# Moving the resident weight tiles 576 bytes down in SBUF, and three small constants behind them

## The reference

```python
for i in range(DEPTH):                      # DEPTH = 2
    h = _rmsnorm(x, g_pre[i])
    o = even_mixer(h) if i % 2 == 0 else odd_mixer(h)
    x = x + _rmsnorm(o, g_post[i])
    x = x + jax.nn.sigmoid(x @ w_ple_gate[i]) * (p[i] @ w_ple[i])
```

## Time and profile before

| | |
|---|---|
| median of 3 runs | 1965.39 us (1963.24 to 1967.23) |
| the profiled execution | 1967.23 us, of which its span (first to last instruction) is 1965.4 us |
| TensorE clock granted, mean | 0.982 of 2.4 GHz |
| PE busy | 1885.1 us, 96% of the span, 9712 matmuls |
| PE weight loads | 1596.0 us, under the matmuls |
| DVE / ACT / POOL busy | 1207.4 / 729.4 / 783.1 us |
| DMA | 302.91 MB moved, 154 GB/s |

### The profile page before, as it was taken

The page is one execution under the profiler, slowest core; times in us unless marked ns, Lnnn a source line. Parts: engine busy times, 40 slices in busy tenths (PEclk is TensorE's granted clock), DMA queues, the critical chain, the costliest instruction groups (busy, mean ns, idle before and its releaser), DMA issues. The chain is left out here.

```text
span 1965.4 us, 26367 instructions
## 1 busy us (share of the span) xinstructions
PE 1885.1 (96%) x9712; PEld 1596.0 (81%) x9712; DVE 1207.4 (61%) x1827; ACT 729.4 (37%) x1471; POOL 783.1 (40%) x540
## 2 busy tenths in 40 slices
PE   4999999999989999999988999999989999999999
PEld 3788888888889788788877888877879889888887
DVE  5499999926678316513754200165667777688886
ACT  6111211211578432212322111122568787445432
POOL 0111121132587553454533322233588975254201
PEclk8999999999999999999989999999989999999999
DMA  4201432453576557544320222286545376557834
GB/s 168 71 11 51 150 99 91 137 170 112 170 251 225 169 170 251 186 131 137 126 63 24 77 86 78 71 335 187 182 153 216 122 259 240 189 192 243 297 128 146
DMA packets 145189, 302.91 MB, mean 154 GB/s; under 512 B 31601, under 2 KB 60017, under 8 KB 145074
## 3 DMA queue, kind: packets, MB, share of 16 engines
q1 hardware_dynamic: 145074, 301.39, 45.6%
HBM read 190.00 MB, written 111.35 MB: 153 GB/s over the span
## 5 line engine op out<-in xcount | busy, mean ns | idle before, releaser
L590 DVE SCALAR_TENSOR_TENSOR ie_acc<-ie_u,ie_wconv,ie_acc 128x1551 f32<-128x1551 f32 x120 | 250.2, 2085 | 3.2
L3039 PE MATMUL og_ps<-w_hi_part,bl_ring 128*128 128x512 f32 x672 | 217.8, 395 | 1.0 <-DVE bl_ring L2572 1.0
L188 POOL TENSOR_TENSOR w_lo_part<-w_raw,w_hi_part 128x1024 fp32r<-128x1024 f32 x24 | 65.3, 2720 | 329.7 <-ACT w_hi_part L180 329.7
L325 PE MATMUL ie_ps<-rows_hi,w_hi_part 128*128 128x512 f32 x384 | 151.0, 393 | 5.0 <-DVE w_lo_part L554 5.0
L325 PE MATMUL ie_ps<-rows_lo,w_hi_part 128*128 128x512 f32 x384 | 150.5, 392 | 0.0
L325 PE MATMUL ie_ps<-rows_hi,w_lo_part 128*128 128x512 f32 x384 | 150.3, 392 | 0.0
L3039 PEld LDWEIGHTS og_ps<-w_hi_part,bl_ring 128*128 128x128 f32 x672 | 126.9, 189 | 27.1 <-DVE bl_ring L2572 1.1
L170 POOL TENSOR_TENSOR w_hi_part<-w_raw,zero 128x1024 fp32r<-128x1024 f32 x40 | 77.7, 1942 | 167.2 <-DMA w_raw<-wall 164.8
L2459 DVE TENSOR_TENSOR mla_pt_lo<-mla_ps_t,mla_pt_hi 128x512 fp32r<-128x512 f32 x160 | 109.2, 687 | 42.2 <-ACT mla_pt_hi L2428 41.3
L3039 PE MATMUL og_ps<-w_lo_part,bl_ring 128*128 128x512 f32 x336 | 131.4, 391 | 0.0
L1859 DVE SCALAR_TENSOR_TENSOR io_stage<-io_tanh,io_ps 128x512 f32<-128x512 f32 x24 | 16.5, 688 | 174.1 <-ACT io_tanh L1817 174.1
(11 more groups left out here) (332 smaller groups left out, 5177.0 us busy)
## 6 DMA issues: line engine op xcount, KB each, us to landing
w_raw<-wall SPq DMA_DIRECT2D x68, 512.0 KB, 4.6
w_hi_part<-weight_blocks SPq DMA_DIRECT2D x28, 512.0 KB, 5.4
w_lo_part<-weight_blocks SPq DMA_DIRECT2D x28, 512.0 KB, 5.6
weight_blocks<-w_hi_part SPq DMA_DIRECT2D x26, 512.0 KB, 7.9
w_flat<-wall SPq DMA_DIRECT2D x16, 512.0 KB, 8.8
weight_blocks<-w_lo_part SPq DMA_DIRECT2D x16, 512.0 KB, 7.3
weight_blocks<-w_raw_rounded SPq DMA_DIRECT2D x14, 512.0 KB, 8.2
pro_x<-x SPq DMA_DIRECT2D x12, 512.0 KB, 8.6
```

What stands on the lines that cost most here:

```text
L325: mm = pe.matmul(psum[:, u % banks], w_at(g, name, a, k * HALF + c * P, P), g.XT[m][:, k, b * 512:(b + 1) * 512], start=i == 0, stop=i == ...
L590: dve.scalar_tensor_tensor(acc[:], ubuf[:, cc, s:s + CW], wconv[:, cc, s:s + 1], acc[:], ALU.mult, ALU.add).then_inc(taps, 1)
L3039: mm = pe.matmul(ps[:, N % 4], bl.part(a, N)[:, k], wb.at(N // HT, m, k), start=k + a + m == 0, stop=k == 3 and a == 1)
```

## The change

`g.W` is now taken with `g.sb` directly behind the staging tile, and `ident`, `zero` and `minus_half` come after it. Before they lay between the two. `g.base`, from which all later tiles are placed, is now computed from the next free offset.

```diff
+        w_at_byte = -(-nc.sbuf_base // 32) * 32
+        g.W = [g.sb("w_hi_part", [P, 2, PAIRCOLS], F32R), g.sb("w_lo_part", [P, 2, PAIRCOLS], F32R)]
+        g.W_flat = [g.region(w_at_byte + 8 * PAIRCOLS * i).sb(f"w_flat{i}", [P, 2, PAIRCOLS]) for i in range(2)]
         g.ident = g.sb("ident", [P, P])
         g.zero = g.sb("zero", [P, 1])
-        g.mhalf = g.sb("minus_half", [P, 1])
-        w_at_byte = -(-nc.sbuf_base // 32) * 32
-        w_at = g.region(w_at_byte)
-        g.W = [w_at.sb("w_hi_part", [P, 2, PAIRCOLS], F32R), w_at.sb("w_lo_part", [P, 2, PAIRCOLS], F32R)]
-        g.W_flat = [g.region(w_at_byte + 8 * PAIRCOLS * i).sb(f"w_flat{i}", [P, 2, PAIRCOLS]) for i in range(2)]
         g.zero3 = g.zero[:].rearrange("p (a b) -> p a b", a=1).broadcast_to([P, NT, DH])
...
+        g.mhalf = g.sb("minus_half", [P, 1])
...
-        g.base = w_at.at
+        g.base = -(-nc.sbuf_base // 32) * 32
```

## The result

The changed kernel is slower: 1984.55 us, median of four runs (1983.84 to 1985.62), against 1965.83 (1963.24 to 1967.23) for four of the kernel before. The ratio is 1.0097, 95% interval 1.008 to 1.0114. The forecast was no change, and its range of 1959 to 1972 does not hold the time. The profiled execution took 1981.16 us with a span of 1979.4, 14.0 us more than the span before.

What follows compares the result with a forecast made beforehand. TensorE, busy 96% of the span, was taken as the bound: matmul count times the distance between starts. Span 1965.4 us plus five terms of 0 gave a median of 1965.4 us, range 1959 to 1972.

Steps and rivals of the forecast that it cites:

- Steps 2 to 5: Transposes, VectorE's convolution steps, POOL's splits with their constant, and DMAs of the weight tiles: each forecast to add 0.
- step 1: TensorE matmuls with a weight tile as operand, at most 5880: 0 ns change each, bounds +6.3 and -13.6 ns.
- first rival: Products of weights and rows: unlike operand starts cost 6.3 ns in each of 5880, 37 us, giving 2002 us; chance 5%.
- Step 4: POOL's splits and the constant they read: 0, bounds 0 and +2 us; only splits at 1398.69 us on the chain.
- Three mixtures and one price: TensorE: 256 column products, transposes and Fourier products with differing start remainders were said to show no price for unlikeness.
- 13.6 ns beside the columns: TensorE: what each 512 column matmul takes (226.9 ns) above its columns' 213.3 ns; said to belong to the matmul.
- second rival: Weight matmuls: the old start at 192 causes their surplus; sparing all 13.6 ns saves 80 us, giving 1885 us; chance 4%.

## Why the prediction was wrong

The view of the bottleneck held: a count of matmuls times the distance between starts, and two thirds of them with a weight tile. Steps 2 to 5 held as well: transposes, DVE, POOL's constant and the DMAs cost nothing. The step that failed is step 1, the value of 0 ns per matmul. It was measured as 2.2 ns where the weights are stationary and 5 to 6.4 ns where they move, 23.4 us of TensorE's time and 18.7 us of the kernel's, inside the stated bounds of -13.6 and +6.3 but at the wrong end. So the first rival was the truth, with a chance of 5%, and its price of 37 us was too high by a factor of two, since matmuls with stationary weights paid a third of it and those of 480 columns and fewer nothing. Step 4 also read the chain too short: after the splits at 1398.69 us it runs through eight more POOL instructions, from 1414.37 us, that write `w_flat`, which is the moved memory. It did no harm, since the mean of its line 2644 is 2382 ns before and after.

Three arguments against that rival did not carry.

- The products of 256 columns and the transposes were taken as tests of unlike operands. They are not: transposes start 95.8 ns apart with their operands alike and 95.7 unlike, and the products of 256 columns in line 2226 went from 119.0 ns alike to 116.4 unlike. "Three mixtures and one price" compared shapes that do not show this price. The only rows of 512 columns with unlike remainders were the latents', and they were slow.
- The attention scores, alike and yet at 396 ns, were read as the same slowness from short groups. Short groups alone do not cost that: line 2257, with groups as short, fell to 227.1 and 227.6 ns as soon as its operands were alike. The scores keep 231 ns in every run here (230.7 to 231.1 on average), and why is open. They stand between products of line 2389 whose operands are unlike in every run (320 and 192 by 512), and lines 1666 and 3069 above are alike groups that rose beside unlike ones, so it may be the same cause at one remove; no run tested that.
- The 13.6 ns beside the columns were rightly put to the matmul and not to its start: no layout brought a line of 512 columns under 226.7 ns on average. The second rival stays refuted. The Trainium skill's figure in "TensorE: Matmul & The Clock Gate", "Back-to-back issue gap", of N/2.4 + 2.5 ns, which that section gives for a matmul by itself and not for a stream with weight loads, was not reached by any line of any run.

The forecast gave 81% to no change on tests of other shapes, while the one test of the right shape was in the profile and said 6.3 ns.

## What to carry to other kernels

Where streams of 512 column matmuls on 4 byte operands bound a kernel, let all moving and stationary tiles start at the same remainder by 256 bytes: 64 bytes off cost up to 6.5 ns in 227 here, 1% of the kernel, and any tile placed before others shifts them. A group of matmuls that is slow from start to start with no wait and no lower clock may lie wrong, which one shifted tile tests. A price is to be read from rows of the same shape; here other shapes pay less of it or none.

## What the runs showed of the hardware

- The distance between starts of 512 column matmuls on `float32r` operands depends on the two operands' offsets by 256 bytes. In lines 325 and 328 it is 226.7 to 227.2 ns alike, 228.9 to 230.0 with the moving one 64 beyond the stationary one, and 233.3 at 64 short, 32 either way and 128 away. Alike is not always that fast: line 1426 has 228.0 to 228.9, and the attention scores have 231.
- At 480 columns it is smaller and has another form: 216.6 to 216.9 ns alike, 215.9 at the change's 64 bytes, up to 219.7 at 128. It is not there at 256 (119.0 alike and 116.4 unlike in line 2226) and 128 (109.7 both ways in line 2193).
- A step of 32 bytes was as bad as 128 (233.3 ns each), and one of 64 nearly so, so starting at multiples of 64 is not enough.
- Leaving one of the high and low weight tiles alike saves nothing (1986.33 and 1988.21 us against 1984.55 with both moved), and with operands unlike the products of a stream take turns at different distances (226.0, 229.1 and 231.7 ns in line 325).
